# The first two of four sums of each unit of weights moved from VectorE to GpSimd, in both down projections of a hybrid encoder block

## The chip, the cores and the metric

One core of a Trainium2 chip runs the whole program. The metric is the device time of one execution in microseconds (us), median of several runs. In the kernel's words TensorE is PE, VectorE DVE, ScalarE ACT, GpSimd POOL and SyncE SP; PEld is TensorE's loading of the stationary operand.

## What is computed

An encoder block on 256 tokens of width 2048, in float32: a half-step feed-forward network (FFN), a mixing part (sparse attention beside a recurrence, one projection in, one out), a second half-step FFN and a last norm. What matters here are the two FFNs:

```python
def swiglu(x, w_gate, w_up, w_down):
    return (jax.nn.silu(x @ w_gate) * (x @ w_up)) @ w_down

h = h + 0.5 * swiglu(rms_norm(h, ffn1_norm[l]), ffn1_w_gate[l], ffn1_w_up[l], ffn1_w_down[l])
...
h = h + 0.5 * swiglu(rms_norm(h, ffn2_norm[l]), ffn2_w_gate[l], ffn2_w_up[l], ffn2_w_down[l])
```

The down projection multiplies 256 x 5632 activations with a 5632 x 2048 matrix.

## The kernel before, in words

**Groups of weights.** All weights come in groups of 128 x 2 x 512 elements (two blocks of 128 rows, 512 columns). SyncE loads each into one of four slots of `raw` (line 388), in a fixed order, when both splits of the group four places earlier are done. ScalarE rounds the group to `whi` (line 401), VectorE takes the rest, `raw` less `whi`, into `wlo` (line 410), and TensorE multiplies: each product of float32 is three matmuls, activations (`hh`, `hl`) by `whi` and `wlo` (line 427, `project_tokens`), 12 matmuls for a plain group. `whi` and `wlo` have four slots too; a split waits for `group_used`, TensorE's count of finished groups. Each engine goes through its own list in order and waits on semaphores.

**Units.** Some pairs of groups, called units, are multiplied with seven block products in place of eight (Strassen's and Winograd's scheme, `unit_products`, line 438): 21 matmuls where two plain groups need 24. For this the columns' sums are formed from the two groups of the unit, before they are split (`unit_sums`): four adds of 128x512 on VectorE (they are recorded at line 1455, the helper `tt`). The second overwrites a half of the unit's second group in `raw`. The sums `col_raw` are then rounded by ScalarE to `col_hi` (line 783, after the fourth sum), and VectorE forms `col_lo` from both. ScalarE may split the unit's second group only after the second sum (it waits for `col_step` 4 * unit + 2). `col_raw` is free for the next unit's sums when `col_lo` is written.

**The order around the change.** `down_order` writes the list of a down projection: for each half of the output's columns (`m`), first plain groups (14, or 6 in the second half), then 7 or 8 units with one or two plain groups between them, then plain groups again (4, or 12 and 10). So there are four stretches with units in the program, 7, 7, 7 and 8 units. VectorE's part of an item of the list is, for a unit, the four sums, the two splits and `col_lo`; for a plain group its split; other work of VectorE (rest of the gate and up products, sums of activations `halves_dve`, turning of x, closing of the first half in `close_pair`) stands between at places written out by hand. In the loops of the gate and up projections there are units as well, with `col_sum` in the place of `col_raw`; they are untouched.

GpSimd issues small loads at the start of the program, and has three memsets in the mixing part (`mix_pool`, lines 1219 to 1222); otherwise it does nothing.

Of the kernel before, what the change touches and what calls it, by code (L numbers as in the profile page):

```python
# [19 lines left out]
ALU = mybir.AluOpType  # L20
# [17 lines left out]
SLOTS = 4  # L38
# [3 lines left out]
FC = F // COLS  # L42
# [7 lines left out]
GATE_TOTAL = GATE_UNITS * (FC - 1)  # L50
# [3 lines left out]
FIRST_UNIT = (0, GATE_TOTAL + sum(UNITS[0]))  # L54
# [27 lines left out]
def down_order(f, m):  # L82

    units, lead, tail = UNITS[f][m], LEAD[f][m], TAIL[f][m]
    plain = [("plain", part, j) for part in range(2) for j in range(units, GF)]
    if not units:
        return plain
    inner = plain[lead:len(plain) - tail]
    items = plain[:lead]
    for i in range(units):  # L90
        items.append(("unit", None, i))
        if i < units - 1:
            items += inner[i * len(inner) // (units - 1):(i + 1) * len(inner) // (units - 1)]
    return items + plain[len(plain) - tail:]
# [18 lines left out]
def down_items(f):  # L113

    items, g = [], 0
    for m in range(2):
        for kind, part, j in down_order(f, m):
            items.append((m, kind, part, j, g))
            g += 2 if kind == "unit" else 1
    return items  # L120
# [36 lines left out]
def build(nc, a, out):  # L157
    with ExitStack() as ctx:
        address = {}

        def sb(name, shape, dt=F32):
            handle = ctx.enter_context(nc.sbuf_tensor(name, shape, dt))
            address[name] = nc.sbuf_base - 4 * int(np.prod(shape[1:]))
            return handle
# [4 lines left out]
        def sem(name):  # L169
            return ctx.enter_context(nc.semaphore(name))  # L170
# [6 lines left out]
        raw = sb("raw", [P, SLOTS, KT, COLS])  # L177
# [27 lines left out]
        def at(name, shape, where, unit=0, plus=0, dt=F32):  # L205
            return nc.alloc_sbuf_tensor_at(name, shape, dt, offset=address[where.name] + unit * UNIT + plus)
# [76 lines left out]
        col_raw = at("col_raw", [P, 3, COLS], consts, plus=4 * P)  # L283
# [30 lines left out]
        PER = 2 * GD  # L314
# [38 lines left out]
        col_step = sem("col_step")  # L353
        col_hi_ready = sem("col_hi_ready")
        col_lo_ready = sem("col_lo_ready")
        unit_used = sem("unit_used")
# [33 lines left out]
        def wait_raw(eng, g, n=0, per=0):  # L390

            extra = 16 * min(max(g // SLOTS + 1 - m0 // SLOTS, 0), GD // SLOTS)
            eng.wait_ge(raw_landed[g % SLOTS], n * (16 * per // SLOTS) + 16 * (g // SLOTS + 1) + extra)
# [9 lines left out]
        def split_lo(base, n, per, j, ncol=COLS):  # L403
            g = base + j
            slot = g % SLOTS

            nc.vector.wait_ge(hi_ready, n * per + g + 1)
            if not (isinstance(n, int) and g + n * per < SLOTS):
                nc.vector.wait_ge(group_used, n * per + g - SLOTS + 1)
            nc.vector.tensor_tensor(wlo[:, slot, :, 0:ncol], raw[:, slot, :, 0:ncol],  # L410
                                    whi[:, slot, :, 0:ncol].bitcast(F32), ALU.subtract).then_inc(lo_ready, 1)
# [366 lines left out]
        def unit_hi(n, unit, col_sum=col_sum):  # L778
# [3 lines left out]
                nc.scalar.wait_ge(unit_used, n * GATE_UNITS + unit)  # L782
            nc.scalar.copy(col_hi[:, :, :], col_sum[:, :, :]).then_inc(col_hi_ready, 1)

        def unit_sums(base, n, per, g, unit, col_sum=col_sum):

            gate, up = (base + g) % SLOTS, (base + g + 1) % SLOTS
            steps = n * (4 * GATE_UNITS)
            wait_raw(nc.vector, base + g, n, per)
            wait_raw(nc.vector, base + g + 1, n, per)  # L790
            if col_sum is col_raw:
                nc.vector.wait_ge(col_lo_ready, unit)
            elif not (isinstance(n, int) and n * GATE_UNITS + unit == 0):
                nc.vector.wait_ge(unit_used, n * GATE_UNITS + unit)
            tt(col_sum[:, 0, :], raw[:, gate, 0, :], raw[:, up, 0, :], ALU.add).then_inc(col_step, 1)
            nc.vector.wait_ge(col_step, steps + (4 * unit + 1))
            tt(raw[:, up, 0, :], raw[:, up, 0, :], raw[:, up, 1, :], ALU.add).then_inc(col_step, 1)
            tt(col_sum[:, 1, :], col_sum[:, 0, :], raw[:, up, 1, :], ALU.add).then_inc(col_step, 1)
            nc.vector.wait_ge(col_step, steps + (4 * unit + 3))
            tt(col_sum[:, 2, :], col_sum[:, 1, :], raw[:, gate, 1, :], ALU.add).then_inc(col_step, 1)  # L800

        def unit_lo(n, unit, col_sum=col_sum):

            if col_sum is col_raw:
                nc.vector.wait_ge(unit_used, unit)
            nc.vector.wait_ge(col_hi_ready, n * GATE_UNITS + (unit + 1))
            tt(col_lo[:, :, :], col_sum[:, :, :], col_hi[:, :, :].bitcast(F32), ALU.subtract).then_inc(col_lo_ready, 1)
# [91 lines left out]
        def ffn_dve(f, base, first_dve):  # L899
# [73 lines left out]
            down = base + FC * PER  # L973
            unit = FIRST_UNIT[f] + GATE_TOTAL
            begin, last_unit = down_places(f)
            for i, (m, kind, part, j, g) in enumerate(down_items(f)):
                if kind == "unit":
                    if unit == FIRST_UNIT[f] + GATE_TOTAL:
                        nc.vector.wait_ge(unit_used, unit)
                    unit_sums(down, 0, 0, g, unit, col_raw)  # L980
                    split_lo(down, 0, 0, g)
                    split_lo(down, 0, 0, g + 1)
                    unit_lo(0, unit, col_raw)
                    unit += 1
                else:
                    split_lo(down, 0, 0, g)
                if i == 1:
                    turned_lo(FC - 2)
                if i == SLOTS - 1:
                    gate_up(FC - 1)  # L990
                if i == SLOTS:
                    turn_quads(FC - 1)
                if i == GD + SLOTS + 1:
                    turned_lo(FC - 1)
                for b, p in enumerate(SUMS_AT):
                    if i == p + 3:
                        halves_lo(hh, hl, hl_sum, act_lo[f], act_hi[f], act_sum[f], b, sum_number(f, b), f)
                    if i in (p, p + 1):
                        halves_dve(hh, hl, hl_sum, act_sum[f], b, sum_number(f, b), f, i == p, i == p + 1)
                if f == 0 and i == last_unit[1] + 5:  # L1000
                    x_lo(1, 1)
                for k in range(2):
                    past = i - last_unit[k] - 5
                    if 0 <= past < 4:
                        close_pair(f, k, 2 * past)
                        close_pair(f, k, 2 * past + 1)
                if i == begin + 3:
                    add_down(f, down, 1)
                if f == 1 and i in (begin + 9, begin + 12):
                    gain_dve((begin + 9, begin + 12).index(i))  # L1010
                if f == 0 and i in (begin + 4, begin + 16, last_unit[1] + 8):
                    turn_x_quads(1, (begin + 4, begin + 16, last_unit[1] + 8).index(i))
                if f == 0 and i == begin + 15:
                    x_lo(1, 0)
# [200 lines left out]
        def mix_pool(pool):  # L1215

            full(pool, "kn", 0)
            stored(pool, "kn", 0)
            pool.memset(tt_all[:, :, :], 0.0).then_inc(tt_zero, 1)
            pool.memset(tinv[:, :], 0.0).then_inc(t_zero, 1)  # L1220
            pool.wait_ge(t_zero, 1)
            pool.memset(tinv[:, 0:1024:33], 1.0).then_inc(t_zero, 1)
# [231 lines left out]
        def tt(out, a0, a1, op):  # L1454
            return V.tensor_tensor(out, a0, a1, op)  # L1455
# [1199 lines left out]
        base2 = FFN_GROUPS + MIX_GROUPS  # L2655
# [22 lines left out]
        @block.gpsimd  # L2678
        def _(pool):
            n = KD  # L2680
            for name in ("mix_norm", "ffn2_norm"):
                pool.dma_start(prow[n:n + KD, :], a[name].rearrange("(k p) -> k p", p=P)).then_inc(const_landed, 16)
                n += KD
            for name in _CHANNELS:
                pool.dma_start(prow[n:n + NT, :], a[name].rearrange("(k p) -> k p", p=P)).then_inc(const_landed, 16)
                n += NT
            for row, col_, name in ((0, 0, "rwkv_mu_w"), (0, 64, "rwkv_mu_a"), (1, 0, "rwkv_mu_g"), (1, 64, "rwkv_mu_g")):
                pool.dma_start(prow2[row:row + 1, col_:col_ + 64], a[name].rearrange("(o n) -> o n", o=1))\
                    .then_inc(const_landed, 16)
            mix_pool(pool)  # L2690

        @block.scalar
        def _(act):
# [147 lines left out]
```

## Time and profile before

| | |
|---|---|
| median of 3 runs | 1835.87 us (1835.83 to 1838.89) |
| the profiled execution's own time | 1837.03 us |
| its span in the profile | 1834.9 us |
| TensorE busy | 1817.6 us (99%) |
| VectorE busy | 1504.9 us (82%) |
| ScalarE busy | 997.4 us (54%) |
| GpSimd busy | 11.1 us (1%) |
| first down projection, its matmuls | from some 480 to 710 us |
| second down projection, its matmuls | from some 1600 to 1828 us |

The span runs from the first to the last instruction of one profiled execution; some 2 us lie around it. Busy times of engines overlap. A row of the order of time gives start, duration, engine, line, what is written from what, how many instructions are merged, and in brackets the idle time before with what ended it ("issue" is a wait for something that the profile doesn't show).

### The profile page before, as it was taken

The numbers are of one execution on the slowest core, as the hardware profiler recorded it, in microseconds if no ns is written. First come the engines' busy times: TensorE is split into PE (matmuls) and PEld (weight loads), VectorE is DVE, ScalarE is ACT, GpSimd is POOL, SyncE is SP. The second block draws the span as 40 slices with busy tenths as digits, with TensorE's granted clock in tenths as the row PEclk, the third lists the DMA queues.
The fourth block names the chain that finished last, engine by engine and source line by source line (L and its number), as shares of the span: only waits on it lengthen the run. The fifth ranks groups of instructions, "written<-read, shape, count | busy, mean of one in ns | idle before, by whom it ended". The sixth has DMA issues, their size and how long they took to land.

```text
span 1834.9 us, 29704 instructions
## 1 busy us (share of the span) xinstructions
PE 1817.6 (99%) x10674; PEld 1544.7 (84%) x10674; DVE 1504.9 (82%) x1754; ACT 997.4 (54%) x1181; POOL 11.1 (1%) x23
## 2 busy tenths in 40 slices
PE   8999999999999999999999999999999999999998
PEld 7888888888888888999998878888888888888886
DVE  5888888888998986688966866688888888899996
ACT  7455555555555655754535665545555555555554
POOL 1000000000000000000000000000000000000000
PEclk9999999999999999999999999999999999999999
DMA  7767776777766778565433558577767677676664
GB/s 239 230 212 222 231 221 206 227 218 233 241 199 210 220 227 266 176 185 143 139 111 108 175 171 264 178 229 234 230 220 233 216 226 225 218 237 199 208 216 149
DMA packets 207850, 380.35 MB, mean 207 GB/s; under 512 B 16016, under 2 KB 35728, under 8 KB 207504
## 3 DMA queue, kind: packets, MB, share of 16 engines
q1 hardware_dynamic: 206768, 377.08, 65.3%
q10 hardware_dynamic: 480, 1.97, 0.3%
q8 instruction: 60, 0.98, 0.2%
q14 instruction: 30, 0.25, 0.0%
q0 software_dynamic: 512, 0.06, 0.0%
HBM read 360.19 MB, written 18.87 MB: 207 GB/s over the span
## 4 chain that ended last, share of the span: by engine, by line
PE 92%; DVE 3%; DMA 2%; ACT 1%; issue 1%; SPq 0%; ACTq 0%; DVEq 0%
PE psA L427 30%; PE psB L427 28%; PE psB L1231 6%; PE psT L438 5%; PE psM L438 5%; PE psA L438 5%; PE psA L1231 4%; PE psB L438 2%; PE psM L427 1%; DVE wlo L410 1%; DMA raw<-in_w_in 1%; PE psA L1242 1%; PE psB L650 1%; DMA raw<-in_ffn_w_down 0%; DVE y L1455 0%
## 5 line engine op out<-in xcount | busy, mean ns | idle before, releaser
L401 ACT CAST whi<-raw 128x1024 fp32r<-128x1024 f32 (+1 forms) x648 | 676.6, 1049 | 693.6 <-DVE raw L1455 186.1
L410 DVE TENSOR_TENSOR wlo<-raw,whi 128x1024 fp32r<-128x1024 f32 (+1 forms) x648 | 771.8, 1214 | 205.2 <-ACT whi L401 192.4
L427 PE MATMUL psA<-whi,xh 128*128 128x512 f32 (+1 forms) x576 | 221.8, 385 | 0.5 <-DVE wlo L410 0.5
L427 PE MATMUL psA<-whi,xl 128*128 128x512 f32 (+1 forms) x576 | 221.2, 384 | 0.0
L427 PE MATMUL psA<-wlo,xh 128*128 128x512 f32 (+1 forms) x576 | 221.2, 384 | 0.0
L427 PE MATMUL psB<-whi,xh 128*128 128x512 f32 x544 | 211.7, 389 | 0.0
L427 PE MATMUL psB<-whi,xl 128*128 128x512 f32 x544 | 211.6, 389 | 0.0
L427 PE MATMUL psB<-wlo,xh 128*128 128x512 f32 x544 | 211.6, 389 | 0.0
L427 PEld LDWEIGHTS psA<-whi,xh 128*128 128x128 f32 x576 | 108.4, 188 | 22.0 <-DVE wlo L410 0.7
L427 PEld LDWEIGHTS psA<-whi,xl 128*128 128x128 f32 x576 | 108.4, 188 | 21.3
L427 PEld LDWEIGHTS psA<-wlo,xh 128*128 128x128 f32 x576 | 108.4, 188 | 21.1
L427 PEld LDWEIGHTS psB<-whi,xh 128*128 128x128 f32 x544 | 102.1, 188 | 21.2
L427 PEld LDWEIGHTS psB<-whi,xl 128*128 128x128 f32 x544 | 102.1, 188 | 21.2
L427 PEld LDWEIGHTS psB<-wlo,xh 128*128 128x128 f32 x544 | 102.1, 188 | 21.2
L1231 PE MATMUL psB<-xh,whi 128*128 128x256 f32 x320 | 92.7, 290 | 0.3 <-DVE wlo L410 0.3
L427 PE MATMUL psA<-whi,hh 128*128 128x512 f32 x236 | 91.8, 389 | 0.0
L427 PE MATMUL psA<-wlo,hh 128*128 128x512 f32 x236 | 91.8, 389 | 0.0
L427 PE MATMUL psA<-whi,hl 128*128 128x512 f32 x236 | 91.8, 389 | 0.0
L1231 PE MATMUL psB<-xh,wlo 128*128 128x256 f32 x320 | 90.5, 283 | 0.0
L1231 PE MATMUL psB<-xl,whi 128*128 128x256 f32 x320 | 90.4, 283 | 0.0
L427 PE MATMUL psB<-whi,hh 128*128 128x512 f32 x220 | 85.6, 389 | 0.0
L427 PE MATMUL psB<-wlo,hh 128*128 128x512 f32 x220 | 85.6, 389 | 0.0
(511 smaller groups left out, 3436.7 us busy)
## 6 DMA issues: line engine op xcount, KB each, us to landing
raw<-in_ffn_w_gate SPq DMA_DIRECT2D x176, 512.0 KB, 4.5
raw<-in_ffn_w_up SPq DMA_DIRECT2D x176, 512.0 KB, 4.6
raw<-in_ffn_w_down SPq DMA_DIRECT2D x176, 512.0 KB, 4.5
raw<-in_w_in SPq DMA_DIRECT2D x80, 512.0 KB, 3.7
raw<-in_w_out SPq DMA_DIRECT2D x32, 512.0 KB, 4.3
quads_dram<-stage SPq DMA_DIRECT2D x88, 128.0 KB, 4.3
stage<-quads_dram SPq DMA_DIRECT2D x22, 512.0 KB, 4.3
x<-in_x SPq DMA_DIRECT2D x4, 512.0 KB, 7.6
```

The source lines that it names most:

```text
L401: nc.scalar.copy(whi[:, slot, :, 0:ncol], raw[:, slot, :, 0:ncol]).then_inc(hi_ready, 1)
L410: nc.vector.tensor_tensor(wlo[:, slot, :, 0:ncol], raw[:, slot, :, 0:ncol], whi[:, slot, :, 0:ncol].bitcast(F32), ALU.subtract).then_inc(l ...
L427: mm = nc.tensor.matmul(ps[:, tb, 0:ncol], lhs[:, k0 + t, tok], rhs[:, slot, t, 0:ncol], start=(first and t == 0 and p == 0 and tb != open ...
L438: mm = nc.tensor.matmul(into, lhs, rhs, start=(start and p == 0), stop=(stop and p == 2))
L650: mm = nc.tensor.matmul(ps[:, tb, :], lhs[:, k0 + j * KT + t, tok], rhs[:, slot, t, :], start=False, stop=(j == SLOTS - 1 and t == KT - 1 ...
L1231: mm = nc.tensor.matmul(ps[:, i * S:(i + 1) * S], w[:, slot, t, ct * P:(ct + 1) * P], h[:, k0 + t, :], start=(first and t == 0 and p == 0 ...
L1242: mm = nc.tensor.matmul(ps[:, at + tb * step:at + tb * step + width], h[:, k0 + t, tok], w[:, slot, t, col:col + width], start=(first and ...
```

## The change

GpSimd computes the first two sums of each unit of both down projections, from a list of its own (`first_sums_pool`), called before and after the memsets of the mixing part. Its first add of a unit waits until both groups have landed and `col_lo` of the unit before is written, the second for the first. VectorE does the last two (`last_sums`), after waiting for GpSimd's second. Who waits for which count of `col_step` on ScalarE stays as it is.

```diff
+        def first_sums_pool(pool, f):
+
+            unit = FIRST_UNIT[f] + GATE_TOTAL
+            base = f * base2 + FC * PER
+            for m, kind, part, j, g in down_items(f):
+                if kind != "unit":
+                    continue
+                even, odd = (base + g) % SLOTS, (base + g + 1) % SLOTS
+                wait_raw(pool, base + g)
+                wait_raw(pool, base + g + 1)
+                pool.wait_ge(col_lo_ready, unit)
+                if unit == FIRST_UNIT[f] + GATE_TOTAL:
+                    pool.wait_ge(unit_used, unit)
+                pool.tensor_tensor(col_raw[:, 0, :], raw[:, even, 0, :], raw[:, odd, 0, :], ALU.add).then_inc(col_step, 1)
+                pool.wait_ge(col_step, 4 * unit + 1)
+                pool.tensor_tensor(raw[:, odd, 0, :], raw[:, odd, 0, :], raw[:, odd, 1, :], ALU.add).then_inc(col_step, 1)
+                unit += 1
+
+        def last_sums(base, g, unit):
+
+            gate, up = (base + g) % SLOTS, (base + g + 1) % SLOTS
+            wait_raw(nc.vector, base + g)
+            wait_raw(nc.vector, base + g + 1)
+            nc.vector.wait_ge(col_step, 4 * unit + 2)
+            tt(col_raw[:, 1, :], col_raw[:, 0, :], raw[:, up, 1, :], ALU.add).then_inc(col_step, 1)
+            nc.vector.wait_ge(col_step, 4 * unit + 3)
+            tt(col_raw[:, 2, :], col_raw[:, 1, :], raw[:, gate, 1, :], ALU.add).then_inc(col_step, 1)
+
...
-                    unit_sums(down, 0, 0, g, unit, col_raw)
+                    last_sums(down, g, unit)
...
+            first_sums_pool(pool, 0)
             mix_pool(pool)
+            first_sums_pool(pool, 1)
```

VectorE, first down projection, from the end of its first unit to the end of its second, before:

```order
L1455 TENSOR_TENSOR col_lo<-col_raw,col_hi 128x1536 [waits col_hi_ready,unit_used]
L410 TENSOR_TENSOR wlo<-raw,whi 128x1024 [waits group_used,hi_ready] x2
L1455 TENSOR_TENSOR col_raw<-raw 128x512 [waits col_lo_ready,raw_landed3,raw_landed2]
L1455 TENSOR_TENSOR raw<-raw 128x512 [waits col_step]
L1455 TENSOR_TENSOR col_raw<-col_raw,raw 128x512
L1455 TENSOR_TENSOR col_raw<-col_raw,raw 128x512 [waits col_step]
L410 TENSOR_TENSOR wlo<-raw,whi 128x1024 [waits group_used,hi_ready] x2
L1455 TENSOR_TENSOR col_lo<-col_raw,col_hi 128x1536 [waits col_hi_ready,unit_used]
```

The same place after the change:

```order
L1483 TENSOR_TENSOR col_lo<-col_raw,col_hi 128x1536 [waits col_hi_ready,unit_used]
L410 TENSOR_TENSOR wlo<-raw,whi 128x1024 [waits group_used,hi_ready] x2
L1483 TENSOR_TENSOR col_raw<-col_raw,raw 128x512 [waits col_step,raw_landed3,raw_landed2]
L1483 TENSOR_TENSOR col_raw<-col_raw,raw 128x512 [waits col_step]
L410 TENSOR_TENSOR wlo<-raw,whi 128x1024 [waits group_used,hi_ready] x2
L1483 TENSOR_TENSOR col_lo<-col_raw,col_hi 128x1536 [waits col_hi_ready,unit_used]
```

Two of the four sums are gone, and the first that is left waits for `col_step`, GpSimd's count.

GpSimd, after its last small load, now (before, the memsets of the mixing part stood here):

```order
L2716 DMA prow<-in_rwkv_mu_g 1x16x4 x2
L798 ISA
L798 TENSOR_TENSOR col_raw<-raw 128x512 [waits col_lo_ready,unit_used,raw_landed3,raw_landed2]
L800 TENSOR_TENSOR raw<-raw 128x512 [waits col_step]
L798 TENSOR_TENSOR col_raw<-raw 128x512 [waits col_lo_ready,raw_landed3,raw_landed2]
L800 TENSOR_TENSOR raw<-raw 128x512 [waits col_step]
```

The two adds repeat for each unit; the ISA row is a load of code for GpSimd ahead of its first add.

## Rows read from the trace of the kernel before

**Rows 1.** The page's head and its busy times.
```profile
span 1834.9 us, 29704 instructions
...
PE 1817.6 (99%) x10674; PEld 1544.7 (84%) x10674; DVE 1504.9 (82%) x1754; ACT 997.4 (54%) x1181; POOL 11.1 (1%) x23
```

**Rows 2.** Busy time in 510:581, 600:674, 1628:1700 and 1720:1797, all four together.
```profile
sum 294.00, PE 294.00 PEld 243.01 DVE 272.98 ACT 170.85 POOL 0.00; mean PE 73.50 PEld 60.75 DVE 68.24 ACT 42.71 POOL 0.00
```

**Rows 3.** Order of time of TensorE where the first unit begins.
```profile
517.37 0.39 PE L427 MATMUL psA<-whi,hl 128*128 128x512 f32 x1
517.60 0.39 PE L438 MATMUL psT<-whi,hh 128*128 128x512 f32 x1
```

**Rows 4.** Order of time of VectorE, from the second unit to the third.
```profile
521.83 0.69 DVE L1455 TENSOR_TENSOR col_raw<-raw 128x512 f32<-128x512 f32 x1 [1.02 <-issue]
522.55 0.69 DVE L1455 TENSOR_TENSOR raw<-raw 128x512 f32<-128x512 f32 x1
523.16 1.41 DVE L1455 TENSOR_TENSOR col_raw<-col_raw,raw 128x512 f32<-128x512 f32 x2
524.49 2.36 DVE L410 TENSOR_TENSOR wlo<-raw,whi 128x1024 fp32r<-128x1024 f32 x2
526.76 1.75 DVE L1455 TENSOR_TENSOR col_lo<-col_raw,col_hi 128x1536 fp32r<-128x1536 f32 x1
528.43 2.35 DVE L410 TENSOR_TENSOR wlo<-raw,whi 128x1024 fp32r<-128x1024 f32 x2
531.88 0.69 DVE L1455 TENSOR_TENSOR col_raw<-raw 128x512 f32<-128x512 f32 x1 [1.09 <-issue]
```

**Rows 5.** SyncE's load of the third unit's second group; us to landing.
```profile
526.92 0.37 SPq L388 DMA_DIRECT2D raw<-in_ffn_w_down  x1
...
raw<-in_ffn_w_down SPq DMA_DIRECT2D x1, 512.0 KB, 4.9
```

**Rows 6.** By tile, four stretches in turn: ns min/median/max, first and last start.
```profile
L1455 DVE TENSOR_TENSOR col_lo<-col_raw,col_hi x7: 1751/1752/1755, 516.8 to 577.4; 128x1536 fp32r<-128x1536 f32 x7
L438 PE MATMUL psM<-col_hi,act_hi x7: 389/389/389, 520.3 to 581.5; 128*128 128x512 f32 x7
...
L1455 DVE TENSOR_TENSOR col_lo<-col_raw,col_hi x7: 1751/1753/1754, 609.3 to 672.8; 128x1536 fp32r<-128x1536 f32 x7
L438 PE MATMUL psM<-col_hi,act_hi x7: 389/389/438, 613.5 to 675.0; 128*128 128x512 f32 x7
...
L1455 DVE TENSOR_TENSOR col_lo<-col_raw,col_hi x7: 1752/1753/1754, 1635.5 to 1697.1; 128x1536 fp32r<-128x1536 f32 x7
L438 PE MATMUL psM<-col_hi,act_hi x7: 389/389/389, 1639.0 to 1700.2; 128*128 128x512 f32 x7
...
L1455 DVE TENSOR_TENSOR col_lo<-col_raw,col_hi x8: 1751/1754/1760, 1727.0 to 1792.9; 128x1536 fp32r<-128x1536 f32 x8
L438 PE MATMUL psM<-col_hi,act_hi x8: 389/389/389, 1732.2 to 1798.1; 128*128 128x512 f32 x8
```

**Rows 7.** Order of time of GpSimd from 700 to 1100: its larger memsets.
```profile
793.37 1.82 POOL L1219 MEMSET tt_all<- 128x2048 f32 x1 [784.10 <-DVE hstat L1809]
795.13 0.95 POOL L1220 MEMSET tinv<- 128x1024 f32 x1
```

**Rows 8.** First and last unit (of nine) whose data waited: load, landing, VectorE.
```profile
506.22 0.37 SPq L388 DMA_DIRECT2D raw<-in_ffn_w_down  x1
...
raw<-in_ffn_w_down SPq DMA_DIRECT2D x1, 512.0 KB, 3.6
...
511.85 0.69 DVE L1455 TENSOR_TENSOR col_raw<-raw 128x512 f32<-128x512 f32 x1
...
1746.41 0.37 SPq L388 DMA_DIRECT2D raw<-in_ffn_w_down  x1
...
raw<-in_ffn_w_down SPq DMA_DIRECT2D x1, 512.0 KB, 4.5
...
1751.33 0.69 DVE L1455 TENSOR_TENSOR col_raw<-raw 128x512 f32<-128x512 f32 x1
```

## The prediction

> **What bounds the kernel now.** I read first the page's head and its table of busy time, then the busy times of the stretches with units, and last the order of time of one unit. TensorE is busy for 1817.6 of 1834.9 us, GpSimd for 11.1 us [rows 1]. In the four stretches of the down projections that hold the units TensorE never waits: its busy time equals their length, 294.00 of 294.00 us, with VectorE busy for 272.98 and GpSimd for none [rows 2]. Its matmuls start 0.227 us apart, from a plain group into a unit too [rows 3]. So work taken from VectorE can gain nothing in these stretches: there is no wait of TensorE to shorten. What can change is the other direction: how late the operands may come before TensorE has to wait.
>
> One unit on VectorE, in order of time [rows 4]: four sums from 521.83 us, the last one over at 524.57; two wlo splits until 526.85; col_lo until 528.51; two plain splits until 530.78; then VectorE is idle for 1.09 us and the next unit begins at 531.88. What it waits for is the second group of that unit: its load was issued at 526.92, right after the second split, and took 4.9 us to land, at 531.8 [rows 5]. So the round is a loop through one buffer slot: landing, four sums, two splits, issue, landing, of 10.05 us. TensorE needs for one unit and two plain groups 21 + 24 matmuls of 0.227 us, 10.2 us. The loop is only 0.15 us faster than its user. The stock that covers a delay is what lies between the end of col_lo and the first matmul that reads it: for the last unit of each stretch 577.4 + 1.75 against 581.5 is 2.35 us, 672.8 + 1.75 against 675.0 is 0.45, 1697.1 + 1.75 against 1700.2 is 1.35, and 1792.9 + 1.75 against 1798.1 is 3.45; 7.6 us together [rows 6].
>
> **The change, part by part.**
> 1. VectorE loses two of four sums in each of 29 units (7, 7, 7 and 8): the last sums start 1.33 us after the first in the rows (521.83 to 523.16) [rows 4], so 29 x 1.34 = 39 us less work. By itself worth nothing, as TensorE has no wait.
> 2. GpSimd gets 58 adds of 128x512. The trace has no add on it, only memsets: 1.82 us for 2048 elements and 0.95 for 1024, so 0.87 us per 1024 elements and about 0.08 fixed [rows 7]. Lower bound: an add as dear as a memset of 512, 0.52 us. Two passes would be 0.95, three passes (two operands read, one written) 1.38, which I take as the upper end. An add has three streams, so three passes is the nearer row; some of the writing should overlap, so I take 1.25 us.
> 3. Two new handoffs. Its second add waits for the end of its first; VectorE's second sum, behind the same kind of wait, starts 0.03 us after the end of its first (521.83 + 0.69 to 522.55) [rows 4]; for GpSimd I take 0.1. Then GpSimd to VectorE, for which I take 0.05. VectorE started its sums 0.08 us after the landing. From landing to the last two sums: 0.08 + 1.25 + 0.1 + 1.25 + 0.05 = 2.73 us. Before it was x + 1.34, where x is how long the landed data waited for VectorE.
> 4. So a unit comes later by 2.73 - 1.34 - x = 1.39 - x. In 20 of the 29 units VectorE had been waiting, x is 0.08 and the unit is 1.31 later. In nine it came late, since other work stood in front of it: in the first unit the load issued at 506.22 landed after 3.6 us at 509.8, and the sums began at 511.85, x = 2.0, behind a split and the split of hl (line 924); in the last of the nine 1746.41 + 4.5 against 1751.33, x = 0.4 [rows 8]. Read in the same way, the nine are 2.0, 0.85, 2.2, 2.0, 1.9, 2.3, 0.4, 0.8 and 0.4, together 12.8. Here GpSimd does its adds while VectorE is busy, and the relief is real: a unit at 2.0 comes 0.6 us earlier.
> 5. ScalarE's split of the second group waits for the second add (it must read the summed data) and moves by the same amount, as do col_hi behind it, both splits, col_lo, SyncE's wait for the slot and its next load. Nothing overtakes anything: the delay goes round the loop and adds up within a stretch. VectorE, waiting for GpSimd, holds the split of the unit's first group though that group is ready; that is what makes the delay whole.
> 6. GpSimd's other work doesn't collide: its memsets begin at 793.37, after the first down projection, and end before the second [rows 7]. SyncE's and ScalarE's orders are as before. The load of GpSimd's code that now stands ahead of its first add is issued before the adds' waits, with some 500 us to spare; were it paid at the first add instead, one unit would be late by it, once.
>
> The sum: 29 x 1.39 = 40.3 us, less all x (20 x 0.08 + 12.8 = 14.4) is 25.9 us of lateness; the stock covers 7.6 of it. **TensorE waits about 18.3 us**: some 4.1, 4.7, 3.5 and 5.9 in the four stretches. The plain groups between stretches refill the stock (TensorE takes 12 x 0.227 = 2.7 us for one, VectorE half of 2.36, 1.2 [rows 4]), so each starts anew, and a wait once taken isn't won back, because TensorE has no other idle time to give. Profiled execution: 1834.9 + 18.3 = 1853.2 span, with 2.1 around it 1855.3; its own time, 1837.03, stands 1.2 above the median shown. Against that median: 1835.9 + 18.3 = **1854.2 us**, 1.0% more.
>
> By the price the Trainium skill gives in GPSIMD Engine Reference, section 3.1 (an add of 2048 elements in 4497 ns, about 2.6 cycles an element), an add here would be an estimated 1.17 us and the sum 13.7 instead of 18.3.
>
> The price decides, since it counts 58 times: 1.0 us gives 3.8 us of waiting, 1.38 gives 25.8, and below about 0.9 TensorE never waits.
>
> **Rivals.**
> - *An add on GpSimd is nearly as cheap as its memset* (0.52 us), or as VectorE's own 0.69 [rows 4]. From landing to the last sums it then takes 1.3 to 1.6 us instead of 1.42, the 20 tight units move by at most 0.2, the nine others come earlier, and TensorE goes on without a wait: 1835.9, no change. It decides below some 0.9 us per add. For it: a memset's rate. Against it: a memset reads nothing. This is the case on the other side. 0.12.
> - *GpSimd and VectorE don't run side by side.* The trace never shows both at work on SBUF here, GpSimd being at 0.00 busy [rows 2]. If a GpSimd add has to wait until VectorE's operation of two SBUF operands is over, or the reverse, then the adds aren't hidden in six of the nine units, those where wlo splits, hl splits or halves of sums stand in front, as in the first of [rows 8]; there the unit is 1.31 later like the rest. That adds their x, 7.8, less 6 x 0.08: 7.3 us, 25.6 in all, 1861.5. For it: nothing in rows; against it neither. 0.30. The Trainium skill, SBUF — State Buffer, section "Who interferes with whom", states it: a VectorE instruction with two SBUF inputs and a GpSimd instruction that reads SBUF exclude each other for the whole instruction. No run here shows it yet.
> - *VectorE's relief speeds the program up.* It would need waits of TensorE in these stretches, and the busy times of the stretches leave no room for one. 0.03.
> - The diff doing something else than it says, or GpSimd's adds above 1.4 us with the time past 1868: 0.05.
>
> **How the numbers follow.** The forecast has 0.50, no overlap 0.30, cheap adds 0.12, faster 0.03, other 0.05. Measurements of this kernel can tell about 0.2%, 3.7 us. Faster 0.03; same 0.12; slower the rest, 0.85. The range runs from adds of 1.0 us with overlap (1835.9 + 3.8 = 1840) to 1.38 without overlap (1835.9 + 25.8 + 7.3 = 1869, I take 1868).
>
> **What would show it.** In the changed kernel's profile: GpSimd with 58 adds near 1.25 us; VectorE about 39 us less busy; VectorE idle before its first sum of a unit for some 2.4 us, released by GpSimd; loops of 11.3 us and not 10.05 inside a stretch; TensorE with waits of 1 to 1.3 us each, for wlo or col_lo, from the third or fourth unit of a stretch on, about 18 us together, and none elsewhere; waits growing in number towards a stretch's end. It is wrong if TensorE still shows no wait in the down projections, if the waits begin with the first unit of a stretch, if adds in the nine busy units take far longer than in the others (then it is the second rival), or if time is lost outside the down projections.

## The result: 1.85% slower, nearly twice the forecast

| | before | after |
|---|---|---|
| median | 1837.38 us (4 runs, 1835.83 to 1840.04) | 1872.15 us (4 runs, 1869.88 to 1873.72) |
| ratio | | 1.0185, 95% interval 1.0169 to 1.0200 |

The change costs 34.8 us; 18.3 were forecast, and the time lies above the range of 1840 to 1868 us. (The median before is of four runs here, 1.5 us above the median of three that the forecast started from.) The page of the changed kernel, head and busy times, beside [rows 1]:

```profile
span 1871.5 us, 29737 instructions
...
PE 1826.3 (98%) x10674; PEld 1540.2 (82%) x10674; DVE 1475.3 (79%) x1696; ACT 992.8 (53%) x1181; POOL 91.5 (5%) x81
```

VectorE has 58 instructions less but only 29.6 us less busy time, where 58 sums of 0.69 us would be 40. A part of the difference is time in which VectorE was held up in the middle of its work; how much, memsets_1408 shows below. GpSimd's adds, in the groups by line (count, busy us, mean ns, idle before and what ended it):

```profile
L798 POOL TENSOR_TENSOR col_raw<-raw 128x512 f32<-128x512 f32 x29 | 40.6, 1402 | 1607.7 <-DMA raw<-in_ffn_w_down 1607.7
L800 POOL TENSOR_TENSOR raw<-raw 128x512 f32<-128x512 f32 x29 | 39.8, 1373 | 2.3
```

The stretches with units, each some microseconds longer than in [rows 2] for the same units (columns: start:end, length, then busy us and count of PE, PEld, DVE, ACT, POOL, clock, DMA share, GB/s). TensorE, which had no idle time there, has some now, and VectorE is idle for a quarter of the time:

```profile
510.00:588.00 78.00, 72.99 (x315) 57.96 (x314) 57.12 (x61) 38.33 (x37) 19.46 (x14) 1.00 0.56 179
600.00:680.00 80.00, 73.64 (x316) 58.05 (x316) 60.41 (x61) 40.76 (x45) 17.20 (x12) 1.00 0.64 199
1640.00:1720.00 80.00, 75.50 (x326) 59.94 (x325) 61.90 (x64) 39.09 (x39) 18.50 (x14) 1.00 0.59 191
1740.00:1827.00 87.00, 80.27 (x345) 63.62 (x344) 62.02 (x59) 43.00 (x45) 19.52 (x15) 1.00 0.56 177
```

One round of the loop, GpSimd and then VectorE in order of time, to be laid beside [rows 4]:

```profile
522.05 1.28 POOL L798 TENSOR_TENSOR col_raw<-raw 128x512 f32<-128x512 f32 x1 [8.91 <-DMA raw<-in_ffn_w_down]
523.40 1.28 POOL L800 TENSOR_TENSOR raw<-raw 128x512 f32<-128x512 f32 x1
533.41 1.29 POOL L798 TENSOR_TENSOR col_raw<-raw 128x512 f32<-128x512 f32 x1 [8.73 <-DMA raw<-in_ffn_w_down]
```

```profile
524.82 1.42 DVE L1483 TENSOR_TENSOR col_raw<-col_raw,raw 128x512 f32<-128x512 f32 x2 [3.58 <-POOL raw L800]
526.15 2.35 DVE L410 TENSOR_TENSOR wlo<-raw,whi 128x1024 fp32r<-128x1024 f32 x2
528.42 1.75 DVE L1483 TENSOR_TENSOR col_lo<-col_raw,col_hi 128x1536 fp32r<-128x1536 f32 x1
530.09 2.36 DVE L410 TENSOR_TENSOR wlo<-raw,whi 128x1024 fp32r<-128x1024 f32 x2
536.20 1.42 DVE L1483 TENSOR_TENSOR col_raw<-col_raw,raw 128x512 f32<-128x512 f32 x2 [3.76 <-POOL raw L800]
```

The first sum starts when the data lands, as before, but the last two start 2.8 us after it (522.05 to 524.82) and not 1.3. The loop takes 11.4 us (522.05 to 533.41), and TensorE's work for it 10.2. So TensorE waits at the next unit for the first split; the order of time of TensorE there:

```profile
537.62 0.39 PE L427 MATMUL psB<-whi,hl 128*128 128x512 f32 x1
538.90 0.47 PE L438 MATMUL psT<-whi,hh 128*128 128x512 f32 x1 [0.89 <-DVE wlo L410]
539.21 0.40 PE L438 MATMUL psT<-wlo,hh 128*128 128x512 f32 x1
```

The starts are 1.28 us apart instead of 0.227. From such distances all of TensorE's waits can be added up by stretch (what a distance above 0.26 us has over 0.227). In microseconds:

```
                first  second  third  fourth stretch | all
before            0.0     0.3    0.0     0.0         |  0.3
after             6.6     9.7    7.2    10.0         | 33.4
```

That is nearly the whole difference of the spans, 36.6 us (one execution each); some 2.7 more lie where the mixing part begins. Each row is one execution, and one stretch can differ by 1 to 2 us between executions of the same instructions (the second stretch has 9.7 here and 8.1 in only_first below). The loads are not the reason: from issue to landing, those of the 29 units' second groups took 4.61 us in the mean before and 4.63 after.

What was not foreseen in the size stands in the first unit. GpSimd and VectorE there, in order of time:

```profile
509.50 1.94 POOL L798 TENSOR_TENSOR col_raw<-raw 128x512 f32<-128x512 f32 x1 [500.22 <-DMA raw<-in_ffn_w_down]
511.52 1.62 POOL L800 TENSOR_TENSOR raw<-raw 128x512 f32<-128x512 f32 x1
```

```profile
509.08 1.22 DVE L410 TENSOR_TENSOR wlo<-raw,whi 128x1024 fp32r<-128x1024 f32 x1
510.21 3.48 DVE L952 TENSOR_TENSOR hl<-stage,hh 128x512 fp32r<-128x512 f32 x2
513.61 1.40 DVE L1483 TENSOR_TENSOR col_raw<-col_raw,raw 128x512 f32<-128x512 f32 x2
```

The adds take 1.94 and 1.62 us instead of 1.28, and the two hl splits together 3.48 instead of some 1.3. Both engines are slower while both work on pairs of SBUF operands. In the kernel before, the last two sums of this unit were 0.4 us earlier, though its second group landed 0.5 us later (at 509.85 and not 509.37):

```profile
513.18 1.41 DVE L1455 TENSOR_TENSOR col_raw<-col_raw,raw 128x512 f32<-128x512 f32 x2
```

Where VectorE transposes instead (one operand), a GpSimd add takes 1.30 us, as if alone; the next one, beside a split, 2.15:

```profile
610.51 1.30 DVE L531 STREAM_TRANSPOSE stage<-x 128x512 f32<-128x512 f32 x2
611.73 1.34 DVE L410 TENSOR_TENSOR wlo<-raw,whi 128x1024 fp32r<-128x1024 f32 x1
```

```profile
610.69 1.30 POOL L798 TENSOR_TENSOR col_raw<-raw 128x512 f32<-128x512 f32 x1 [28.33 <-DMA raw<-in_ffn_w_down]
612.07 2.15 POOL L800 TENSOR_TENSOR raw<-raw 128x512 f32<-128x512 f32 x1
```

In another unit VectorE is the one that comes second, and it is held: an act_sum, 0.42 us alone, takes 1.40, and a split of 1.22 us takes 2.30, each nearly to the end of the add beside it.

```profile
1705.85 1.40 DVE L1483 TENSOR_TENSOR act_sum<-act_sum 128x256 f32<-128x256 f32 x1
1707.18 2.30 DVE L410 TENSOR_TENSOR wlo<-raw,whi 128x1024 fp32r<-128x1024 f32 x1
```

```profile
1705.55 1.41 POOL L798 TENSOR_TENSOR col_raw<-raw 128x512 f32<-128x512 f32 x1 [8.83 <-DMA raw<-in_ffn_w_down]
1707.05 1.35 POOL L800 TENSOR_TENSOR raw<-raw 128x512 f32<-128x512 f32 x1
```

Three theories were left. **A, lateness alone**: two slow adds in a loop with 0.15 us to spare; with the measured 1.28 us and handoffs, 29 x (2.89 - 1.34) - 14.4 - 7.6 = 22.9 us (2.89 from the landing to the last two sums). **A with exclusion**: the same, and a GpSimd add that reads SBUF and a VectorE operation with two SBUF inputs keep each other waiting. **B**: a cost of the handoff or of GpSimd's work as such, wherever it stands.

### The profile page after: what moved, and what is told of

It reads as the page before. It is cut to its first block, busy times and chain, and to the rows that moved or that the text cites. A ratio compares the mean times of both kernels' runs of the same rounds, so it can differ in the third digit from the quotient of the medians.

```text
span 1871.5 us, 29737 instructions
## 1 busy us (share of the span) xinstructions
PE 1826.3 (98%) x10674; PEld 1540.2 (82%) x10674; DVE 1475.3 (79%) x1696; ACT 992.8 (53%) x1181; POOL 91.5 (5%) x81
## 4 chain that ended last, share of the span: by engine, by line
PE 81%; DVE 6%; DMA 6%; issue 3%; POOL 2%; ACT 2%; SPq 0%; POOLq 0%; DVEq 0%; ACTq 0%
PE psA L427 27%; PE psB L427 24%; PE psB L1259 6%; DMA raw<-in_ffn_w_down 5%; PE psT L438 4%; PE psM L438 4%; PE psA L438 4%; PE psA L1259 4%; DVE wlo L410 2%; PE psB L438 2%; POOL col_raw L798 1%; PE psM L427 1%; POOL raw L800 1%; ACT whi L401 1%; DVE col_raw L1483 1%
## 5 line engine op out<-in xcount | busy, mean ns | idle before, releaser
L798 POOL TENSOR_TENSOR col_raw<-raw 128x512 f32<-128x512 f32 x29 | 40.6, 1402 | 1607.7 <-DMA raw<-in_ffn_w_down 1607.7
L1483 DVE TENSOR_TENSOR col_raw<-col_raw,raw 128x512 f32<-128x512 f32 x58 | 40.1, 692 | 88.1 <-POOL raw L800 87.1
```

The costliest lines, as they stand in the source:

```text
L798: pool.tensor_tensor(col_raw[:, 0, :], raw[:, even, 0, :], raw[:, odd, 0, :], ALU.add).then_inc(col_step, 1)
```

## The experiments

### Each down projection by itself

```diff
-                    last_sums(down, g, unit)
+                    if f == 0:
+                        last_sums(down, g, unit)
+                    else:
+                        unit_sums(down, 0, 0, g, unit, col_raw)
...
-            first_sums_pool(pool, 1)
```

> The two first sums on GpSimd in the first down projection alone, the second as before. Theory A (lateness adds up inside each stretch and the stretches are independent): the waits of the first down projection in the changed kernel's trace are 6.4 and 9.3 us in its two stretches, with some 2 us more where the mixing part begins, so 1837.4 + 18 = 1855. Rival B (something outside the stretches, for instance GpSimd's code load or a general slowdown, takes part of the 35 us): clearly more or less than half, and the two halves don't add up to 35.

> The same in the second down projection alone. Theory A: the waits in its two stretches are 7.0 and 9.6 us in the changed kernel's trace, so 1837.4 + 16.6 = 1854, and no new wait in the first down projection or at the start of the mixing part. Rival B: as for the first, the halves don't add up.

Measured: 1853.51 us (ratio 1.0088, 1.0071 to 1.0105) for the first alone, 1855.26 us (1.0092, 1.0075 to 1.0108) for the second alone, against 1838.09 before on the same chip: 15.4 and 17.2 us. The sum is 32.6, the two together cost 34.8. TensorE's waits by stretch:

```
only_first        6.8     8.1    0.0     0.0         | 14.9
only_second       0.0     0.6    7.0     9.2         | 16.9
```

The costs lie in the stretches that were changed, and the others stay within 0.6 us of none. Both halves load GpSimd's code; a fixed cost of the program would be in each and would make their sum larger than 34.8, which it is not.

### The price of an add and what it reads

Both adds of a unit replaced by memsets of GpSimd, with all waits as they are. The memsets write into `col_raw` and read nothing. These kernels leave out the first two sums of each unit, so they don't compute the product; they serve for the time alone.

```diff
-                pool.tensor_tensor(col_raw[:, 0, :], raw[:, even, 0, :], raw[:, odd, 0, :], ALU.add).then_inc(col_step, 1)
+                pool.memset(col_raw[:, :, :].rearrange("p k c -> p (k c)")[:, 0:1408], 0.0).then_inc(col_step, 1)
                 pool.wait_ge(col_step, 4 * unit + 1)
-                pool.tensor_tensor(raw[:, odd, 0, :], raw[:, odd, 0, :], raw[:, odd, 1, :], ALU.add).then_inc(col_step, 1)
+                pool.memset(col_raw[:, :, :].rearrange("p k c -> p (k c)")[:, 0:1408], 0.0).then_inc(col_step, 1)
```

> Both GpSimd adds of a unit are replaced by memsets of 128x1408 into col_raw, by the memsets in the trace 1.28 us each, as long as an add alone; so the first two sums are not computed. Every wait stays. They write but read nothing. Theory A with exclusion (only a GpSimd operation that reads SBUF collides with VectorE's two inputs): the lateness of 2.9 us stays, the collisions in six units go: 29 x (2.89 - 1.34) - 14.4 - 7.6 = 22.9 us, 1860, and no VectorE operation longer than before. If there is no exclusion, or if writes collide as well: as the changed kernel, 1872.

> As memsets_1408 with 128x1024, 0.95 us each; the first two sums are not computed. From landing to the last two sums 0.12 + 0.95 + 0.08 + 0.95 + 0.12 = 2.22 us. Theory A: 29 x (2.22 - 1.34) - 14.4 - 7.6 = 3.5 us, 1840 to 1841. If the waits were in proportion to the duration (25 us at 1.28 each, nothing at 0.52), it would be 25 x (0.95 - 0.52) / (1.28 - 0.52) = 14 us, 1851.

> The same with memsets of 128x512, 0.52 us each; the first two sums are not computed. From landing to the last two sums 0.12 + 0.52 + 0.08 + 0.52 + 0.12 = 1.36 us, under the 1.42 of the kernel before. Theory A: TensorE has no wait in the down projections, 1837. Rival: the handoff to another engine itself (its semaphores, VectorE idle) costs whatever the price of an add: well above 1837.

| kernel | each, us | time | ratio | over the runs of before beside it |
|---|---|---|---|---|
| memsets_512 | 0.53 | 1836.49 us | 0.9999 (0.9990 to 1.0009) | none |
| memsets_1024 | 0.96 | 1846.36 us | 1.0043 (1.0029 to 1.0057) | 8.5 us |
| memsets_1408 | 1.28 | 1862.36 us | 1.0136 (1.0119 to 1.0153) | 25.3 us |
| the change | 1.28 alone, 1.39 mean | 1872.15 us | 1.0185 (1.0169 to 1.0200) | 34.8 us |

```
memsets_512       0.0     0.0    0.0     0.0         |  0.0
memsets_1024      0.0     5.7    1.0     3.4         | 10.1
memsets_1408      3.5     8.6    3.9     9.4         | 25.4
after             6.6     9.7    7.2    10.0         | 33.4
```

Three things follow. A handoff costs only the lateness it brings: with 0.53 us each, the last two sums start 1.34 us after the landing (1.42 in the kernel before), VectorE has 34 us less to do (busy for 1471.1 us), and the time is that of the kernel before, neither slower nor faster. So the relief is worth nothing, and B falls. There is a threshold: the cost from 0.53 to 0.96 us is 8.5, from 0.96 to 1.28 another 17. And it counts that the adds read: with memsets of 1.28 us, 9.5 us less are lost by the medians (34.8 against 25.3) and 8.0 by TensorE's waits, and these are missing in the first and third stretches above all (3.1 and 3.3 us), where the hl splits and the halves of sums stand in front of units. Some 2 of them are not the reading: from landing to the last two sums it is 2.84 us with these memsets and 2.91 with undisturbed adds, 29 times. The first unit in memsets_1408, VectorE and GpSimd, to be laid beside 3.48 and 1.94 above:

```profile
509.29 1.29 DVE L952 TENSOR_TENSOR hl<-stage,hh 128x512 fp32r<-128x512 f32 x2
511.31 1.42 DVE L1483 TENSOR_TENSOR col_raw<-col_raw,raw 128x512 f32<-128x512 f32 x2 [0.73 <-POOL col_raw L800]
```

```profile
508.56 1.28 POOL L798 MEMSET col_raw<- 128x1408 f32 x1 [499.31 <-DMA raw<-in_ffn_w_down]
509.90 1.28 POOL L800 MEMSET col_raw<- 128x1408 f32 x1
```

Neither engine is held up. VectorE is busy for 1467.8 us in this kernel, 7.5 less than in the changed one with the same instructions on it: that is the time in which it was held. The time is 1862.4 where lateness alone gave 1860. The expectation for 0.95 us was too low, 3.5 against 8.5, and the second stretch alone makes the difference: 5.7 where the working gives 1.0. A part of it can be seen in SyncE's order of time, in memsets_1024 at the end of that stretch:

```profile
641.31 5.89 SPq L388 DMA_DIRECT2D raw<-in_ffn_w_down  x3
648.00 5.40 SPq L540 DMA_DIRECT2D xq_dram<-stage  x8
653.49 7.38 SPq L388 DMA_DIRECT2D raw<-in_ffn_w_down  x5
```

The eight stores of turned x stand in SyncE's list between two loads of weights, and take 5.4 us to issue. A unit that comes early in front of them gives its gain away, since the next load waits for the stores and not for the unit. The working had passed such gains on. Besides, the load of the next unit, which runs beside these stores, took 7.1 us to land where it had been 6.5 in the kernel before (5.4 to 7.8 in the kernels here), and TensorE's longest wait of this kernel, 3.0 us, follows it. How the 4.7 us divide, and how much of them is scatter between executions, was not tried.

### Adds that nobody waits for

VectorE does all four sums as in the kernel before; GpSimd works beside it on other data, from the landing of each unit on, in the second down projection alone.

```diff
+                for side_step in range(4):
...
+                    pool.tensor_tensor(side, twice, twice, ALU.add).then_inc(t_zero, 1)
```

`twice` is `prow` read twice, `side` the tile `token_scale`, which is dead by then. In side_memsets the line is `pool.memset(token_scale[:, :], 0.0)`, eight times.

> VectorE does all four sums as in the kernel before. GpSimd does four adds of 128x256 of unrelated data per unit (reading prow, writing a dead tile), about 0.7 us each, from the landing of the unit's groups on; nobody waits for them; second down projection alone, 15 units. Exclusion: VectorE's four sums and GpSimd's four adds take turns, the sums take up to 2.7 us longer, 1855 to 1870, with VectorE's sums recorded at over 1 us. No exclusion: 1837, sums at 0.69 us.

> As side_adds, with eight memsets of 128x256 (0.3 us each) in the place of the four adds: GpSimd is as long busy but reads nothing. Both theories: 1837 and sums at 0.69 us. If writes of GpSimd hold VectorE too: above 1850.

Measured: side_adds 1857.01 us (1.0102, 1.0085 to 1.0119), side_memsets 1837.52 us (1.0005, 0.9995 to 1.0014). In the order of time of side_adds, VectorE and GpSimd:

```profile
1665.93 0.69 DVE L1486 TENSOR_TENSOR col_raw<-raw 128x512 f32<-128x512 f32 x1 [0.90 <-issue]
1666.65 0.98 DVE L1486 TENSOR_TENSOR raw<-raw 128x512 f32<-128x512 f32 x1
1667.56 2.12 DVE L1486 TENSOR_TENSOR col_raw<-col_raw,raw 128x512 f32<-128x512 f32 x2
1669.60 2.76 DVE L410 TENSOR_TENSOR wlo<-raw,whi 128x1024 fp32r<-128x1024 f32 x2
```

```profile
1665.97 4.18 POOL L803 TENSOR_TENSOR token_scale<-prow 128x256 f32<-128x256 f32 x4 [7.10 <-DMA raw<-in_ffn_w_down]
```

and in side_memsets:

```profile
1640.21 0.69 DVE L1484 TENSOR_TENSOR col_raw<-raw 128x512 f32<-128x512 f32 x1 [1.09 <-issue]
1640.93 0.69 DVE L1484 TENSOR_TENSOR raw<-raw 128x512 f32<-128x512 f32 x1
1641.55 1.41 DVE L1484 TENSOR_TENSOR col_raw<-col_raw,raw 128x512 f32<-128x512 f32 x2
```

```profile
1640.22 2.90 POOL L801 MEMSET token_scale<- 128x256 f32 x8 [8.99 <-DMA raw<-in_ffn_w_down]
```

No instruction waits for these adds or memsets, and yet the adds make VectorE's four sums take 3.75 us (1665.93 to 1669.68) instead of 2.75 and the two splits behind them 2.76 instead of 2.36, so that the loop takes 11.3 us, and the program 20 us longer; the memsets cost nothing. So the exclusion is shown by itself, without any handoff. It goes with reading as far as these kernels tell: the memsets kept GpSimd busy for 2.90 us at each unit without holding anything, but they are another operation than an add, and a GpSimd operation with a single read was not tried. Nor is the exclusion whole in time for such short adds: four adds and four sums finish within 4.2 us, while the sums alone are 2.75 and four times the shortest recorded add (0.63 us) is 2.5, together 5.3. So the recorded time of an add has a part that leaves VectorE alone.

### VectorE fills its wait with the unit's first split

```diff
-                    last_sums(down, g, unit)
                     split_lo(down, 0, 0, g)
+                    last_sums(down, g, unit)
...
+                    freed[g + SLOTS] = 4 * unit
...
+                        sp.wait_ge(col_step, freed[at_])
```

> Two adds on GpSimd, but VectorE splits the unit's first group before it waits for GpSimd (the load into that slot then waits for the unit's last sum). If GpSimd and VectorE can work side by side, the split is hidden behind the adds: landing to the end of both splits is 2.89 + 1.33 + 1.2 = 5.4 us against 5.2 in the kernel before, and nearly all is won back: 1838 to 1842. If a GpSimd add and a split (two SBUF inputs) exclude each other, the split fits only between or before the adds and pushes them back by its 1.2 us: 6.6 us as now, 1870 to 1873.

Measured: 1869.41 us (1.0172, 1.0155 to 1.0189), 31.3 us over the kernel before, with waits of 5.5, 8.9, 7.8 and 10.2 us. The remedy that looks right by lateness alone wins 3.5 of 34.8 us. GpSimd and VectorE there, in the second unit of the first stretch:

```profile
522.18 1.80 POOL L806 TENSOR_TENSOR col_raw<-raw 128x512 f32<-128x512 f32 x1 [9.15 <-DMA raw<-in_ffn_w_down]
524.06 1.28 POOL L808 TENSOR_TENSOR raw<-raw 128x512 f32<-128x512 f32 x1
```

```profile
521.61 1.22 DVE L410 TENSOR_TENSOR wlo<-raw,whi 128x1024 fp32r<-128x1024 f32 x1
525.47 1.42 DVE L1491 TENSOR_TENSOR col_raw<-col_raw,raw 128x512 f32<-128x512 f32 x2 [2.64 <-POOL raw L808]
526.81 1.22 DVE L410 TENSOR_TENSOR wlo<-raw,whi 128x1024 fp32r<-128x1024 f32 x1
528.51 1.76 DVE L1491 TENSOR_TENSOR col_lo<-col_raw,col_hi 128x1536 fp32r<-128x1536 f32 x1 [0.49 <-ACT col_hi L791]
```

The split runs from 521.61 to 522.83 and holds the first add, which takes 1.80 us instead of 1.28. The last two sums start 3.3 us after GpSimd begins instead of 2.8 (525.47 - 522.18 against 524.82 - 522.05). Behind them a second chain has become the last: VectorE is idle for 0.49 us before `col_lo`, waiting for `col_hi`, and `col_lo` ends at 530.27, 8.1 us after GpSimd began, as late as in the changed kernel (530.17 after 522.05). The waits of TensorE say the same:

```profile
PE psM L438 <- DVE col_lo L1491: 10.5, 23, 0.6
```

So it now waits 23 times for `col_lo`, 10.5 of the 19.9 us of idle time that this view gives it in the down projections (the rest is for `wlo`); in the changed kernel it never waited for `col_lo`. The exclusion takes 0.5 us of the gain in a unit of the first stretch and up to 1.0 in the second (last two sums 3.4 and 3.5 to 3.9 us after the landing, 2.9 in the changed kernel), as expected in kind but less in size (1.2). In the unit shown the chain of `col_hi` and `col_lo`, which the expectation had left out, takes the rest. In the first stretch the waits do fall, from 6.6 to 5.5 us; why they rise in the third and fourth is not settled.

### One add instead of two

GpSimd does the first sum alone, VectorE the other three (its list gets `tt(raw[:, up, 0, :], raw[:, up, 0, :], raw[:, up, 1, :], ALU.add)` back).

> GpSimd does the first sum alone, VectorE the other three. From landing to the last two sums: 0.12 + 1.29 + 0.1 + 0.72 = 2.23 us instead of 1.42 before and 2.89 with two adds. Theory A with overlap: 29 x (2.23 - 1.34) - 14.4 - 7.6 = 3.8 us, 1841. Theory A with exclusion of GpSimd's adds and VectorE's operations with two SBUF inputs: up to 7.3 us more, 1841 to 1849. If the time were a price per unit regardless of lateness, it would be half of 35 us: 1855.

Measured: 1850.65 us (1.0067, 1.0050 to 1.0084), 12.6 us more than before, with 1.2, 6.8, 2.3 and 3.7 us of waits. The last two sums begin 2.04 us after the add (521.55 to 523.59), where 2.11 were expected (2.23 from the landing, less 0.12 until the add begins). The time lies a little above the upper end, 1849, though not by more than the interval (1847 to 1854 us), and far above 1841 for overlap. The price per unit regardless of lateness, 1855, lies outside the interval. As with the memsets of 1024, the second stretch has the most.

### Only the units whose data had waited for VectorE

```diff
+LATE = [FIRST_UNIT[0] + GATE_TOTAL + u for u in (0, 7, 11)] + [FIRST_UNIT[1] + GATE_TOTAL + u for u in (0, 5)]
...
-                    last_sums(down, g, unit)
+                    if unit in LATE:
+                        last_sums(down, g, unit)
+                    else:
+                        unit_sums(down, 0, 0, g, unit, col_raw)
```

> GpSimd does the first two sums only in the five units whose groups had waited 1.9 us or more for VectorE in the kernel before (the first of three stretches, the fifth of the second, the sixth of the third); in the other 24 VectorE does all four. Theory A: each of them comes up to 0.6 us earlier where transposes stand in front (two units) and up to 1.5 us later where operations with two SBUF inputs do (three units), which the stock of 1.3 to 1.9 us covers: 1837 to 1838, no change, and no gain either, since TensorE has no wait to lose. If a handoff to GpSimd costs TensorE something wherever it stands: 5/29 of 35 us, 6 us more, 1843.

Measured: 1837.90 us against 1837.87 (1.0001, 0.9992 to 1.0010), with 0.1 us of waits in all four stretches. The ten adds, in the groups by line:

```profile
L804 POOL TENSOR_TENSOR raw<-raw 128x512 f32<-128x512 f32 x5 | 8.9, 1778 | 0.4
L802 POOL TENSOR_TENSOR col_raw<-raw 128x512 f32<-128x512 f32 x5 | 7.6, 1529 | 1507.7 <-DMA raw<-in_ffn_w_down 1507.7
```

They cost nothing where the stock is full, though their means are 1.53 and 1.78 us, and win nothing. Of the kernels that compute the whole product none beats the kernel before.

## Why the prediction was wrong, point by point

- **What bounds the kernel.** Right. TensorE had nothing to win, which memsets_512 shows with 34 us of VectorE's time taken away and no gain; the loop through the slot with 0.15 us to spare is what breaks (10.05 us before, 11.4 after, 11.3 forecast).
- **Step 2, the price of an add.** 1.25 us was taken; the 40 adds of the 20 units in which VectorE had been waiting take 1.29 us in the median. Nearly right; 58 x 0.04 is 2.2 us. The estimate of 1.17 us from the figure in the Trainium skill's GPSIMD Engine Reference, section 3.1, is low by 0.12.
- **Step 3, the handoffs.** From landing to the last two sums 2.73 us was forecast; it is 2.89 in the round shown and 2.91 in the median: 0.12 until GpSimd starts, 1.37 from add to add, 1.42 from the second add's start to VectorE. That is 0.18 us for each of 29 units, 5.2 us: 2.2 from the price in step 2 and 3.0 from the handoffs, 0.33 us together where 0.23 was taken. Undersized.
- **Step 4, nine units in which GpSimd's adds are hidden.** This is the step that failed. It let VectorE's splits and sums and GpSimd's adds run side by side, so that the nine units would come 0.3 us early in total (9 x 1.39 - 12.8). From landing to the start of the last two sums, the nine took 24.8 us together before and 33.5 after, 8.7 us late. With 2.91 us each they would have taken 26.2; the other 7.3 us are the time in which the two engines held each other up, the largest single error of the forecast. In the first unit, forecast 0.6 us early, the load landed at 509.37 and the last two sums started at 513.61, 4.2 us later; before, it was 509.85 and 513.18, 3.3 us; so it came 0.9 us late. The second rival, 1861.5 with chance 0.30, had the true mechanism. The Trainium skill, SBUF — State Buffer, section "Who interferes with whom", states it: a VectorE instruction with two SBUF inputs contends with a GpSimd instruction that reads SBUF. The traces agree in which operations collide (VectorE's sums and splits with GpSimd's adds, not with its memsets; not VectorE's transposes). The prediction's "for the whole instruction" is nearly true beside adds of 128x512 (the act_sum above waited 0.98 of the 1.11 us that its add had left) and not beside the adds of 128x256 in side_adds. The rival had been given less weight than the overlap, for which no row spoke either. That it too came to 7.3 us is in part luck: it held six of the nine units back in full and three not at all, while in the trace eight of them were held, by 0.2 to 1.3 us, also the two behind transposes (0.87 us each), since a split follows the transposes and meets the second add.
- **The sum.** The lateness over all 29 units, from landing to the last two sums, was forecast as 25.9 us; the two traces give 38.5, and 25.9 + 5.2 for step 3 + 7.3 for step 4 is 38.4. Less the stock of 7.6 that is 30.9 us. TensorE waited 33.1 us more than before in the stretches and 2.7 elsewhere; the profiled executions differ by 36.3 us and the medians by 34.8. So some 2 us in the stretches stay unexplained, and memsets_1408, where nothing collides, has such a rest too (29.2 - 7.6 = 21.6 by its trace, 25.4 measured). The stores in SyncE's list may be one reason in the second stretch; for the fourth none was looked for.
- **"Each stretch starts anew, none elsewhere."** Nearly: each half costs mainly in its own stretches. In the changed kernel's trace 2.7 us more were lost where the mixing part begins. The changed first down projection doesn't explain them by itself: only_first lost 0.6 us more there than the kernel before, and only_second, with that projection as it was, 1.5. This stays open.
- **Signs named beforehand.** TensorE's first wait of more than 0.2 us came at the second unit in three stretches and at the third in the first one, earlier than the third or fourth unit of the forecast; in six of the nine busy units one of the two adds took 1.8 to 2.2 us, the sign named for the second rival; VectorE's busy time fell by 29.6 us and not 39, and 7.5 us of the difference is time in which it was held (the rest is missing with the memsets too, and was not looked for).
- **The range.** Its upper end took the dearest adds and the exclusion together, 25.8 + 7.3 = 33.1 us over 1835.9, rounded down to 1868. The cost is 34.8 us over 1837.4. The handoffs, fixed at a guess, had no upper end of their own; 3.0 us of the cost are theirs.

## What to carry to other kernels

Before moving work off a busy engine, find the loop in which it stands and compare the loop's length with the time of the engine that bounds: VectorE was 93% busy in the stretches, yet the landing of the data set the pace, and a slower helper that starts at the same moment only lengthens the loop. Such a cost has a threshold and then comes back with every round (nothing at 0.53 us an operation, 25 us at 1.28). GpSimd adds beside VectorE operations on two SBUF operands are to be counted as taking turns with them, nearly in full at 128x512 and about half of the adds' time at 128x256 (1.4 of 2.5 us in side_adds).

## What the hardware showed that was not expected

- GpSimd adds of 128x256 that nobody waits for made three of VectorE's four sums take 0.98 to 1.10 us instead of 0.69 and the program 20 us longer; eight memsets of 0.31 us at each unit left them at 0.69.
- A pair of hl splits of 0.69 us each took 3.48 us beside two GpSimd adds, while these took 1.94 and 1.62 us instead of 1.28: both engines lose. Where an act_sum met an add that had begun, it waited for most of what was left of it.
- GpSimd's add of 128x512 takes 1.28 to 1.29 us alone, 1.35 to 1.37 from start to start with a semaphore between; a memset of 128x1408 takes 1.28.
